# First group's keys and values as fp32 products, tile by tile, inside the input norm of a decoder trunk

## The reference

```python
xn = rmsnorm(x, ln1_g)
u, v, q, k, va, ga, gb = split(xn @ w_in)        # 1024 x 5632, one projection
a = gelu(u) * (tril(W_s) @ rmsnorm(gelu(v)) + b_s)
b = sliding_window_attention(q, k, va, sinks)    # 16 query heads, 4 key/value heads of 64
x = x + (sigmoid(ga) * (a @ w_oa) + sigmoid(gb) * (b @ w_ob)) @ w_out
x = x + relu(rmsnorm(x, ln2_g) @ w_up)**2 @ w_down
y = rmsnorm(x, lnf_g)
```

## Time and profile before

| | |
|---|---|
| median of 3 runs | 1582.38 us (1581.19 to 1582.66) |
| the profiled execution's own time | 1578.94 us |
| its span | 1576.9 us |
| mean granted TensorE clock | 0.989 of 2.4 GHz |
| PE busy | 1539.6 us, 98% of the span |
| DVE, ACT, POOL busy | 1072.8, 759.0, 184.9 us |
| PE's share of the chain that ended last | 89% |

### The profile page before, as it was taken

The page is one execution under the profiler, slowest core; times in us unless marked ns, Lnnn a source line. Parts: engine busy times, 40 slices in busy tenths (PEclk is TensorE's granted clock), DMA queues, the critical chain, the costliest instruction groups (busy, mean ns, idle before and its releaser), DMA issues.

```text
span 1576.9 us, 28772 instructions
## 1 busy us (share of the span) xinstructions
PE 1539.6 (98%) x12226; PEld 1505.6 (95%) x12226; DVE 1072.8 (68%) x1386; ACT 759.0 (48%) x1159; POOL 184.9 (12%) x206
## 2 busy tenths in 40 slices
PE   5999999999999999999999999999999999999998
PEld 5988989899999989999999999999999999999997
DVE  7476575303777567866778676977697769776975
ACT  6466565423635535555443645434543354345533
POOL 7122322100000010000020130000000000000001
PEclk8999999999999999999999999999999999999999
DMA  8612011215695523636597364545454545454612
GB/s 229 202 30 64 19 32 40 87 49 154 168 313 144 161 55 103 166 87 174 115 280 176 107 134 134 135 133 135 129 135 116 140 122 141 120 144 117 152 41 108
DMA packets 106406, 200.59 MB, mean 127 GB/s; under 512 B 16624, under 2 KB 44272, under 8 KB 98952
## 3 DMA queue, kind: packets, MB, share of 16 engines
q1 hardware_dynamic: 89344, 127.64, 24.3%
q0 software_dynamic: 10384, 64.00, 20.8%
q10 hardware_dynamic: 6552, 7.13, 1.4%
HBM read 121.77 MB, written 19.30 MB: 89 GB/s over the span
## 4 chain that ended last, share of the span: by engine, by line
PE 89%; DVE 4%; DMA 3%; issue 2%; ACT 1%; POOL 1%; SPq 0%; ACTq 0%; DVEq 0%; POOLq 0%
PE ps L1596 68%; PE ps L1384 12%; PE ps L1372 3%; PE ps L1453 2%; PE ps L1435 2%; DMA raw<-in_w_in 1%; DMA h_t<-h_keep 1%; DVE y_t L1361 1%; PE ps L1574 1%; DMA wbuf<-wbuf 1%; PE ps L1516 1%; DMA cv<-in_cache_v_win 1%; DMA xn_keep<-xg 0%; DVE vn L1296 0%; DVE xg L999 0%
## 5 line engine op out<-in xcount | busy, mean ns | idle before, releaser
L1596 PE MATMUL ps<-xp_hi,wp_hi 128*128 128x258 f32 x3136 | 887.6, 283 | 4.1 <-DVE wp_lo L1160 2.9
L1596 PE MATMUL ps<-xp_hi,wp_lo 128*128 128x258 f32 x3136 | 886.7, 283 | 0.0
L1596 PE MATMUL ps<-xp_lo,wp_hi 128*128 128x258 f32 x3136 | 886.3, 283 | 0.0
L1596 PEld LDWEIGHTS ps<-xp_hi,wp_hi 128*128 128x128 f32 x3136 | 594.3, 190 | 6.1 <-DVE wp_lo L1160 3.6
L1596 PEld LDWEIGHTS ps<-xp_lo,wp_hi 128*128 128x128 f32 x3136 | 593.2, 189 | 0.0
L1596 PEld LDWEIGHTS ps<-xp_hi,wp_lo 128*128 128x128 f32 x3136 | 592.5, 189 | 0.0
L701 ACT ACTIVATE wp_hi<-wbuf 128x1024 fp32r<-128x1024 f32 x196 | 207.7, 1059 | 539.8 <-PE ps L1596 533.7
L1160 DVE TENSOR_TENSOR wp_lo<-wbuf,wp_hi 128x1024 fp32r<-128x1024 f32 x196 | 243.4, 1242 | 165.0 <-ACT wp_hi L701 165.0
L1384 PE MATMUL ps<-xn_hi,w_hi 128*128 128x344 f32 x480 | 160.2, 334 | 3.1 <-DVE xn_lo L1004 1.9
L1384 PE MATMUL ps<-xn_hi,w_lo 128*128 128x344 f32 x480 | 155.0, 323 | 0.0
L1384 PE MATMUL ps<-xn_lo,w_hi 128*128 128x344 f32 x480 | 154.9, 323 | 0.0
(11 more groups left out here) (192 smaller groups left out, 1559.7 us busy)
## 6 DMA issues: line engine op xcount, KB each, us to landing
wbuf<-wbuf POOLq DMA_DIRECT2D x57, 1024.0 KB, 7.9
wbuf<-in_w_up SPq DMA_DIRECT2D x24, 1024.0 KB, 5.5
wbuf<-in_w_down SPq DMA_DIRECT2D x24, 1024.0 KB, 5.1
wbuf<-in_w_in SPq DMA_DIRECT2D x18, 1024.0 KB, 5.5
raw<-in_w_in SPq DMA_DIRECT2D x40, 256.0 KB, 3.3
wbuf<-in_w_ob SPq DMA_DIRECT2D x6, 1024.0 KB, 7.1
wbuf<-in_w_oa SPq DMA_DIRECT2D x6, 1024.0 KB, 5.1
wbuf<-in_w_out SPq DMA_DIRECT2D x6, 1024.0 KB, 10.3
```

Source lines behind the costliest of these rows:

```text
L1596: last = mm(ps[:, 2 * p + b, 0:HN], w[:, (2 * n + p // 2) % 2, k, p % 2 * P:(p % 2 + 1) * P], x[n % 2][:, k, b * HN:(b + 1) * HN], start=( ...
```

## The change

Job 0 is no longer made from split numbers. Its weights go to `kv_raw` (which lies over slot 0 of `w_hi`), with no copy to fp32r and no subtraction, and a new function `keys_values(t)` of PE makes the products of one tile, in plain fp32, directly from `xg` after `scale_x`: 8 products per tile, 72 in all, in place of 72 products of 344 rows. `xg` has five buffers; a buffer is free when its low part, its keys and values and its store are done. The products stand in banks 7, 1 and 5, three tiles to a bank. The norm's spread has bank 6 alone, so `spread(t)` waits for `scale_x(t-1)` where it waited for `scale_x(t-2)`. The tiles 0 to 4 are worked on behind the turns of tiles 5 to 8; tiles 5 and 6 behind the last two spreads; tiles 7 and 8 after them. The pieces of banks that stood in this place are now job 1's. Job 1's weights are loaded right behind job 0's, and job 2's after the stores of tiles 0 to 2. `w_high(2)` waits for all nine tiles (`kv_done`), since it writes over `kv_raw`. Before the first queries and the first probabilities are written, ACT and DVE wait for the stores that read the `xg` buffers beneath them.

```diff
-        xg = place("xg", [P, 3, KT, P], F32, r_2 + 4 * D)
+        kv_raw = place("kv_raw", [P, KT, P], F32, r_whi)
+        XS, XB = 5, 4 * KT * P
+        xg = [place(f"xg{n}", [P, KT, P], F32, at_) for n, at_ in enumerate(
+            [r_2 + 4 * D + XB * n for n in range(3)] + [r_s + 1024 + 8 * HPG * P + XB * n for n in range(2)])]
+        def kv_part(n):
+            return ps[:, (7, 1, 5)[n], 0:3 * P if n < 2 else 2 * P + NB]
+        def bank_of(n):
+            return ps[:, n % NT if n != NT + 1 else 4, 0:TN]
...
 # SP
+                if g == 0:
+                    for col, src in halves:
+                        sp.dma_start(kv_raw[:, :, col:col + HD], src).then_inc(kv_in, 16)
+                else:
+                    load(j, s, [(raw[:, s, :, col:col + HD], src) for col, src in halves])
+                load_block(j + 1, 1 - s, w_in, 0, g * 2 * P + OQ)
                 if g == 0:
                     for t in range(3):
                         keep_xn(t)
-                load_block(j + 1, 1 - s, w_in, 0, g * 2 * P + OQ)
+                load_block(j + 2, s, w_in, 0, g * 2 * P + P + OQ)
...
 # POOL
-                if t >= 3:
-                    pool.wait_ge(xn_done, t - 2)
-                    pool.wait_ge(xn_kept[t % 3], 16 * (t // 3))
+                if t >= XS:
+                    pool.wait_ge(xn_done, t - XS + 1)
+                    pool.wait_ge(kv_done, t - XS + 1)
+                    pool.wait_ge(xn_kept[t % XS], 16 * (t // XS))
...
 # ACT
-                if t == 4:
-                    w_high(0)
+                if t == 5:
+                    w_high(1)
+                src = bank_of(n)
+                if j == 0:
+                    cols, src = slice(3 * b * P, min(3 * (b + 1) * P, T)), kv_part(b)
+                    act.wait_ge(kv_done, 3 * (n + 1))
-            w_high(1)
...
 # PE
-                if t >= 2:
-                    pe.wait_ge(xn_ready, t - 1)
-                spread_rstd(ps[:, 6 + t % 2, 0:ROWS[t]], t).then_inc(rstd_spread, 1)
+                if t >= 1:
+                    pe.wait_ge(xn_ready, t)
+                spread_rstd(ps[:, 6, 0:ROWS[t]], t).then_inc(rstd_spread, 1)
+            def keys_values(t):
+                r = ROWS[t]
+                if t == 0:
+                    pe.wait_ge(kv_in, 32)
+                pe.wait_ge(xn_ready, t + 1)
+                for k in range(KT):
+                    last = mm(kv_part(t // 3)[:, t % 3 * P:t % 3 * P + r], kv_raw[:, k, :], xg[t % XS][:, k, 0:r],
+                              start=(k == 0), stop=(k == KT - 1))
+                last.then_inc(kv_done, 1)
...
+                for e in {5: (0,), 6: (1, 2), 7: (3,), 8: (4,)}.get(t, ()):
+                    keys_values(e)
                 if t >= 7:
-                    bank(0, 0, 0, 0, ready=3, ks=range((t - 7) * KT // 2, (t - 6) * KT // 2))
+                    bank(1, 3, 1, 0, ready=3, ks=range((t - 7) * KT // 2, (t - 6) * KT // 2))
             spread(NTOK - 2)
-            bank(0, 1, 0, 1, ready=6, ks=range(KT // 2))
+            keys_values(5)
+            bank(1, 4, 1, 1, ready=6, ks=range(KT // 2))
             spread(NTOK - 1)
-            bank(0, 1, 0, 1, ks=range(KT // 2, KT))
+            keys_values(6)
+            bank(1, 4, 1, 1, ks=range(KT // 2, KT))
+            keys_values(7)
+            keys_values(8)
...
-            for n in range(2, 3 * NT - 1):
+            for n in range(NT + 2, 3 * NT - 1):
                 filler(n)
```

More of the change, by code:

```diff
@@ L215, in build_trunk @@
         xp_lo = [place(f"xp_lo{n}", [P, MH, HT], F32R, at_ + 4 * MH * HT) for n, at_ in enumerate((r_3, r_s + 4 * T))]
-        tmp = place("tmp", [P, D], F32, r_s + 4 * T)
+        tmp = place("tmp", [P, D], F32, o)
+        XS, XB = 5, 4 * KT * P
+        assert 4 * D + 3 * XB <= 4 * HPG * T and 2 * XB <= 8 * HPG * SW
+        xg = [place(f"xg{n}", [P, KT, P], F32, at_) for n, at_ in enumerate(
+            [r_2 + 4 * D + XB * n for n in range(3)] + [r_s + 1024 + 8 * HPG * P + XB * n for n in range(2)])]
         ps = ctx.enter_context(nc.psum_tensor("ps", [P, 8, 512], F32))
@@ L268, in build_trunk @@
         vs_stored = sem("vs_stored")
-        xn_kept = [sem(f"xn_kept{n}") for n in range(3)]
+        xn_kept = [sem(f"xn_kept{n}") for n in range(XS)]
+        kv_in, kv_done = sem("kv_in"), sem("kv_done")
         xn_in = {(kh, th): sem(f"xn_in{kh}{th}") for kh in range(2) for th in range(2)}
@@ L423, in keep_xn @@
                 sp.dma_start(xn_keep[:, toks(t)].rearrange("(k p) t -> p k t", p=P),
-                             xg[:, t % 3, :, 0:ROWS[t]]).then_inc(xn_kept[t % 3], 16)
+                             xg[t % XS][:, :, 0:ROWS[t]]).then_inc(xn_kept[t % XS], 16)
             for g in range(NG):
                 j, s = 3 * g, g % 2
-                load(j, s, [(raw[:, s, :, half * HD:(half + 1) * HD],
-                             w_in[:, g * HD + col:(g + 1) * HD + col].rearrange("(k p) n -> p k n", p=P))
-                            for half, col in ((0, OK), (1, OVA))])
+                halves = [(half * HD, w_in[:, g * HD + col:(g + 1) * HD + col].rearrange("(k p) n -> p k n", p=P))
+                          for half, col in ((0, OK), (1, OVA))]
+                if g == 0:
[4 more added lines that the diff above has]
+                load_block(j + 1, 1 - s, w_in, 0, g * 2 * P + OQ)
                 if g == 0:
@@ L711, in w_high @@
             def w_high(j):
-                act.wait_ge(w_loaded[j % 2], j // 2 * 32 + 32)
-                if j >= 2:
+                act.wait_ge(w_loaded[j % 2], j // 2 * 32 + j % 2 * 32)
+                if j == 2:
+                    act.wait_ge(kv_done, NTOK)
+                elif j > 2:
                     act.wait_ge(job_done, j)
@@ L721, in high @@
                 act.wait_ge(xn_ready, t + 1)
-                copy(xn_hi[:, :, toks(t)], xg[:, t % 3, :, 0:r]).then_inc(xhi_done, 1)
+                copy(xn_hi[:, :, toks(t)], xg[t % XS][:, :, 0:r]).then_inc(xhi_done, 1)
             for t in range(NTOK):
@@ L752, in bank_high @@
                 if pair < 0:
-                    copy(kv_t[par][:, cols], ps[:, b, 0:TN])
+                    copy(kv_t[par][:, cols], src)
                     for half in range(2):
-                        last = copy(k_hi[par][half * HD:(half + 1) * HD, cols], ps[0:HD, b, 0:TN])
+                        last = copy(k_hi[par][half * HD:(half + 1) * HD, cols], src[0:HD, :])
                 else:
                     for half in range(2):
-                        last = copy(q_st[par][0:HD, 2 * pair + half, cols], ps[half * HD:(half + 1) * HD, b, 0:TN])
+                        last = copy(q_st[par][0:HD, 2 * pair + half, cols], src[half * HD:(half + 1) * HD, :])
                 last.then_inc(bank_hi, 1)
@@ L1383, in bank @@
                     for p, (w, x) in enumerate(((w_hi, xn_hi), (w_hi, xn_lo), (w_lo, xn_hi))):
-                        last = mm(ps[:, b, 0:TN], w[:, s, k, :], x[:, k, b * TN:(b + 1) * TN],
+                        last = mm(ps[:, b, 0:TN] if n is None else bank_of(n), w[:, s, k, :], x[:, k, b * TN:(b + 1) * TN],
                                   start=(k == 0 and p == 0), stop=(k == KT - 1 and p == 2))
```

47 lines of the change are left out of this document (28 added, 19 removed).

## The result

The changed kernel took **1572.63 us** in the median of 5 runs (1569.43 to 1574.43), the kernel before 1581.75 in the same runs: ratio 0.994, interval 0.9928 to 0.9952. So it is 9 to 10 us faster, where 6.2 were forecast.

What follows compares the result with a forecast made beforehand. PE, busy 98%, was taken as the bound, with room only in the start. From 18.1 us, 42.9 us of work, lower clock and wait put the first scores at 61.0, not 67.16: 1582.38 - 6.2 = 1576.2 us, range 1572.5 to 1580.7.

Steps and rivals of the forecast that it cites:

- What bounds it: Whole span: PE busy 98%; only the start has room, with PE waiting 8.9 us for DVE's copies and its clock low.
- no hole worth naming: After the first scores at 67.16 us: PE has no notable hole up to the end of the busy part.
- PE's work: Start: job 0's 11.4 us of products replaced by 16.9 us of fp32 products, a loss of 5.5 us in work alone.
- The lower clock: Start, from 18.1 us: clock stays low until 22.8 us, costing half of 4.7, 2.3 us.
- The shift applies to both: End of kernel: the 6.2 us gained at the first scores carries to profiled execution and median, 1582.38 to 1576.2 us.
- the dips: Beyond the start: single clock dips come and go by their place; one such low stretch cost half of 3.4 us.
- the fourth rival: Before first scores: job 3's weights, expected at 56.1 us, land late; at 18 us landing 2.4 us lost; 5%, still faster.
- The buffers: Start: POOL's 2.40 us wait for tile 3's buffer goes, counted as 1.5 us of DVE; new buffer condition met by 2 us or more.
- Job 2's weights: Start: issued 20 us earlier, ending the 14 us landing that made the old 1.2 us hole; 0.8 us of wait left.
- The rival of a low clock: Start: turns and fp32 products don't raise the clock; up to 20 us slower; 6% for a loss, 6% for no difference.
- The rule that transposes don't count as PE being busy: Start: skill page's rule on the clock; the prediction said the trace disagrees and let the clock rise at 22.8 us.
- The price of 81 ns: Keys' and values' products: skill page's issue gap would make a tile 2.6 us and the sum 67; prediction kept 1.89 us.

Runs made afterwards that it cites:

- tile0_early: Changed kernel with keys' and values' weights loaded ahead of x tiles 5 to 7 and tile 0's products behind the turn of tile 4; 1570.97 us, ratio 0.9939.
- earlier: tail_order plus keys' and values' weights ahead of x tiles 5 to 7, tile 0's products behind tile 4's turn, job 3's weights behind tile 5's store; 1571.31 us.
- filled_loads: Kernel before with unread fp32 products in PE's gaps, and job 2's weights loaded behind the store of tile 4; 1581.49 us, ratio 1.0007.
- twice_2_7: Changed kernel with the keys' and values' products of tiles 2 and 7 made twice; 1582.28 us, ratio 1.0008.
- tail_order: Changed kernel with tiles 7 and 8 directly behind tile 6, ahead of the second half of job 1's second bank; 1569.86 us, ratio 0.9925.
- five_buffers: Kernel before with five row buffers in place of three and nothing else of the change; 1579.89 us, ratio 0.9999.
- before_filled: Kernel before with fp32 products that nobody reads put into PE's gaps; 1582.50 us, ratio 1.0011.
- three_buffers: Changed kernel with three row buffers as before; 1582.81 us, ratio 1.0013.
- job3_early: As tail_order, and job 3's weights loaded behind the store of tile 5 instead of behind the last one; 1571.82 us, ratio 0.9932.

## Why the prediction was right or wrong

**What bounds it** was right for the start: PE's holes and its low clock there. But "no hole worth naming" after the first `scores` was a misreading. In the kernel before, PE stands still for 12.4 us of the 1433 up to 1500 us, and all differences behind the `scores` arise at four places, in each of which PE waits:

```profile
67.00:1500.00 1433.00, 1420.57 (x11373) 1390.82 (x11372) 981.08 (x1284) 696.77 (x1065) 145.97 (x130) 1.00 0.47 125
```

**PE's work** was right: the change adds work (PE is 3.8 us busier), a tile was taken at 1.89 us and cost 1.79, the ninth 1.7 in place of 1.8, a bank about 3.9 in place of 3.80. Nine tiles took 16.5 us with 0.3 of lower clock in them, the forecast was 16.9. Turns and spreads took 4.2 (3.9), the five banks 19.2 (19.0), the hole 0.9 (0.8).

**The lower clock** was the mis-sized term of that sum. "I take the same here, to 22.8 us, which costs half of 4.7: 2.3": the clock rose at 19.6 us. The 4.7 us were counted from 18.1, where PE had been busy from the turn at 16.75; but it rose 2.8 us after that turn, and not 4.9 as before after 26.77, so a right start of the count would have mended part only. Why it is shorter no run shows. Behind 18.7 the clock cost 0.3 us by tile 0's length. Against that, the turn at 16.75 ran at half speed and the sum started at 18.7 instead of 18.1. In the nine profiles that have products or idle products right behind the turn of tile 5 and the clock low there, it rose between 19.6 and 21.9 us and cost up to 1.2 us more, and in tile0_early and earlier it never fell; so 2.3 lay above all that was seen. With this, 61.0 becomes 59.3. That this profile has the earliest rise of them is luck.

**"The shift applies to both"**, the profiled execution and the median, was the step that failed by more. 6.2 were forecast and 7.9 seen at the `scores`, but the runs show 9.1 and 10.0 at the end. Over all runs the forecast of 1576.2 us lies 5.0 above the changed kernel's 1571.2, and three parts of like size make this up. It was built on 1582.38, the median of three runs, where 94 give 1580.9: 1.5 us. The `scores` moved 1.7 us more than forecast, or 1.9 by the second profiles. And the end moved 9.7 us where the `scores` moved 7.9 to 8.1: some 1.7 us. So the size of the shift was off by 1.7 us, and carrying it over to the median by 3.2. Of the last part, 0.6 us are less time at the lower clock beyond the start (9.9 against 10.5 us, with a standard error of 0.8). The rest I can't place, and it is hardly more than the noise: the two intervals hold gains from 7.6 to 11.4 and from 8.2 to 12.5 us.

The shift of the `scores` fails to reach the end the other way as well: filled_loads is 3 us ahead at the `scores` and not faster, with 12.1 us lost; twice_2_7 is 3.4 ahead and not faster, with 13.3. With the same products of PE behind the `scores`, the mean span less the first `scores` lies between 1508.8 us (tail_order) and 1516.2 (twice_2_7). The lower clock makes up a part of this: against the kernel before 1.6 of 3.4 us in filled_loads and 2.8 of 4.7 in twice_2_7. The profiles show longer waits of PE beside it, at two of the four places. Near 312 us for a load from the value cache, in five_buffers (its waits of PE from 300 to 345 us; twice_2_7 has 2.4, the others 0.8 to 1.3):

```profile
PE ps L1376 <- DMA cv<-in_cache_v_win: 2.6, 1, 2.6
```

And near 920 us, in filled_loads (here, from 905 to 945 us), before_filled and twice_2_7, a wait with no releaser in the profile, where the others have 0.4 to 0.7:

```profile
PE ps L1567 <- issue: 2.1, 1, 2.1
```

I had treated the dips as a width of the range, centred on nothing. That dips and waits can lean one way for a version, by as much as the change is worth, is likely from these runs; why stays open, since no run moved the long stage without changing the start.

**The late weights** (the fourth rival) were nearer than forecast: landed at 55.3 us as worked out, but 0.5 us of room in place of 1.5, because PE came 1.7 us sooner. **The buffers** I priced as 1.5 us of DVE's time. They are more: three_buffers shows that without them the products in the gaps gain nothing, for their products now hold the buffers. The prediction had this condition "met by 2 us or more", and did not say what it would cost if it weren't. For the single spread bank it was not met by 2 us either: PE waited 0.9 us for it, ahead of 14 us. **Job 2's weights** I priced by the 1.2 us hole. filled_loads shows that they also hid what the clock is worth at the `scores`, so removing either alone would have given little.

**The rival of a low clock** did not come. The rule that transposes don't count as PE being busy (the Trainium skill, "TensorE: Matmul & The Clock Gate", section "Part 4: PE-mode transpose") got no support, though the better evidence is not at tile 5, where fp32 products stand behind the turn. It is at the beginning. In the kernel before, 16 turns of tiles 1 and 2 at 6.83 us took 3.67 us, one spread followed, and the next 8 turns took 1.25 us, then 1.06. In the changed kernel, too, the first 8 took 1.94 us and those at 10.19 took 1.04, with nothing but turns and one spread between. This stands on durations alone: the windows of both profiles print a granted clock of 1.00 up to 16 us, the slow first turns included, so they show no rise.

```profile
6.83 3.67 PE L1372 MATMUL ps<-ident,x_stage 128*128 128x128 f32 x16 [0.22 <-DMA x_stage<-in_x_prompt]
10.73 1.25 PE L1372 MATMUL ps<-ident,x_stage 128*128 128x128 f32 x8
```

**The price of 81 ns** per pass of the same page (section "Back-to-back issue gap") did not hold either: a tile's 16 records took 1.79 us, 56 ns for each of 32 passes if a record stands for two.

## What to carry to other kernels

Work that is dearer on the bound engine can pay, if it can be done while that engine stands still; count the work and then the gaps, not the instructions saved. When several limits lie one behind the other (gaps, clock, a late load, buffers), taking away any one of them shows little, as five_buffers, before_filled and three_buffers do, and all together are 8 us at the mark. Judge a change of half a per cent in such a long kernel by a mark in the trace behind the changed place and by ten runs or more, and don't expect the two to agree to a few us.

## What the hardware showed that I had not expected

The time lost to the lower clock in the long stage came in steps: 1.7 us, 3.4, and 5.1 in filled_loads and twice_2_7, at five places, about 320, 360, 575, 840 and 922 us, of which a profile shows three to five. The last microseconds of every profile cost another 2.0 to 2.7 us. At four of the places PE has just waited, and the same instructions are hit in one execution and not in the next. The one near 360 us is in all fourteen profiles, and there PE has no wait at all. In the kernel before, 64 products of 4 columns stand right ahead of it, and the clock is low from 362.7 to 366.1 us:

```profile
358.51 3.90 PE L1537 MATMUL ps<-dp_t,cv 128*64 128x4 f32 x64
```

Where the next loads of weights (256 KB each) follow the last tile's store at once, between 39 and 48 us and beside the store of 4.1 MB, they landed 11.5 to 14.8 us after their issue, in all such kernels. Behind 60 us such loads landed in 2.8 to 5.0. Job 3's weights issued ahead of the big store, at 30 us in job3_early, took 4.7 to 5.0. Which of the stores costs the time was not taken apart.

DVE's low part of a tile took 2.06 us beside POOL's multiplication of the next tile, and 1.22 us when POOL had only small work left. In the timeline of the changed kernel, DVE:

```profile
33.66 2.06 DVE L1030 TENSOR_TENSOR xn_lo<-xg,xn_hi 128x1024 fp32r<-128x1024 f32 x1
36.87 1.22 DVE L1030 TENSOR_TENSOR xn_lo<-xg,xn_hi 128x1024 fp32r<-128x1024 f32 x1
```

And POOL:

```profile
32.74 1.90 POOL L582 TENSOR_TENSOR xg<-x_t,g 128x1024 f32<-128x1024 f32 x1
36.37 0.29 POOL L582 TENSOR_TENSOR xg<-x_t,g 128x64 f32<-128x64 f32 x1
```

The first low part ends at 35.72, 1.1 us after POOL's step, which ends at 34.64, as if it had stood until then. The Trainium skill, "SBUF — State Buffer", section "SBUF: two separate sides", says that a DVE instruction with two SBUF inputs and a GpSimd instruction that reads SBUF exclude each other for the whole instruction. The trace agrees in these two rows of each. DVE's work with this stall sets the beat of 3.7 us per tile (33.66 less 29.95) which now stands right behind PE.
